# A one-layer hybrid encoder step on eight cores: the division of each attention head in three spread steps, and another plan for the bf16 weight copies

## The chip, the cores and the metric

The kernel runs on all 8 NeuronCores of one Trainium2 chip. Cores 0 to 3 form one die, cores 4 to 7 the other. Each core has a matrix engine (TensorE, PE in the rows), a vector engine (VectorE, DVE), an activation engine (ScalarE, ACT), GpSimd (POOL) and a sync engine (SyncE, SP), and 16 DMA engines that all of its DMA queues share. The metric is the device time in microseconds of the slowest core for one launch. Every core does the same amount of work on its own data; there is no traffic between cores.

## The reference, cut to what matters

One layer is computed for 4 prompts of 8192 frames and 32 running streams of 16 new frames:

```
xn = rms_norm(x);  q,k,v,u,vb,gA,gB = split(xn @ w_in)            # 2048 -> 9216
A  = softmax(q.k/sqrt(128) + bias, own 64-chunk + 8 before) @ v   # 8 heads of 128
S  = gelu(u) * (causal(w_s) @ rms_norm(gelu(vb)) + b_s)           # 128-frame chunks
x  = x + (sigmoid(gA)*(A @ w_branch_a) + sigmoid(gB)*(S @ w_branch_b)) @ w_out
h  = conv3(rms_norm(x) @ w_up);  x = x + (gelu(h_gate)*h_val) @ w_down  # 2 x 5632 wide
y  = rms_norm(x)
```

K and V rows, the normalised rows of the spatial gate and the last rows ahead of the convolution are returned too. All weights arrive as f32.

## The kernel before, in words

**Tiles.** A core takes 4096 prompt frames (half of a prompt, with 576 frames of halo) and 4 of the 32 running streams. It works through its frames in 8 tiles of 512 frames. Tile 0 also carries 66 extra columns (64 frames of the running streams, 2 halo columns), so that most of its matmuls come in two sets of 289 columns where later tiles have one of 512. All activations are feature-major: features on partitions, frames along the free axis. In each tile the stages follow one another: `vb` and `u` with the spatial gate; attention, with q, k, v projections as filler; the merge of both branches (`merge`); the output projection (`out_proj`); the FFN (`ffn`), which does `w_up` in two parts (24 and 20 blocks), each followed by its half of `w_down` (16 blocks each). Tile 0 has the halo and the running streams besides.

**Order of the work.** The class `Sched` records operations in program order, one in-order list for each engine, and derives the semaphore waits from the keys that they read and write. Nothing is reordered: what an engine meets in its list is what it waits for. `mm` (line 394) issues every matmul, `Sched.dma` (line 93) every DMA.

**Weights.** `wload` brings one weight block (up to 128 partitions x 4096 bf16, 1 MiB) into the next slot of a ring `wbuf` of 5 slots; in the FFN of tile 0 the ring has 7 (two in `wx_sb`). There are 136 blocks, numbered `bi` in the order of first use: 0 to 19 are q, k, v, u and vb; 20 to 51 the merge, in fours (gate A, gate B, `w_a`, `w_b`; the last two are 512 KiB); 52 to 59 `w_out`; 60 to 83 and 100 to 119 `w_up` (1 MiB each); 84 to 99 (768 KiB) and 120 to 135 (640 KiB) `w_down`. A block is used once per tile. Until a bf16 copy of it lies in the DRAM scratch `wscr`, it is loaded from the f32 original `wblk` with a casting DMA on GpSimd's queue. Once the copy is there, it is loaded from `wscr` on SP's queue. `keeps(rk, bi, uses)` (line 417) decides at each casting load whether the block is also stored to `wscr` after it has landed: `uses` is 0 in tile 0, 1 in tile 1, and in tile 2 whatever is left is stored. The store is queued on SP two `wload`s later (`flush_stores`), and the next load into the same slot waits for it. The merge asks for blocks in the order gate A, gate B, `w_a`, `w_b`, and uses them in the order gate A, `w_a`, gate B, `w_b`, for each of the two feature chunks of a step; 8 steps make a merge.

**Attention.** `attention_run` walks over 64 items, 8 key blocks for each of 8 heads. An item's front (`attn_front`) is the score matmul, a bias add on VectorE (line 851) and an exponential on ScalarE (line 854) into `pbf`; its back (`attn_back`), two items later, is the product with V into the bank `ob` and the row sum (product with ones) into the bank `db`. Items are 128, 256, 384, 512, 512, 384, 256 and 128 columns wide. Behind the items the generator `fillers` gives out portions of 4 matmuls of the q, k, v and first gate projections, paced by `total`; `ready(h)` pulls q and k of a head ahead of its first item. After a head's last item `finish_head` divides: ScalarE takes Ln of `db` (line 826), copies `ob` (line 827), takes Exp(-Ln) (line 828), and GpSimd multiplies (line 833; VectorE in tile 0). The banks alternate, (6, 7) for even heads and (2, 3) for odd ones. `next_norm` loads the next tile's x in pieces (`xst`, on ScalarE's DMA queue) during the second part of the FFN; its squares (line 490) and their matmuls (`Stats`) stand between the FFN's. `xst` has 2 slots in tile 0 and 4 later.

Of the kernel before, what the change touches and what calls it, by code (L numbers as in the profile page):

```python
# [207 lines left out]
def build(n_main=8, do_ext=True):  # L208
    nc = bass.Bass("TRN2", target_bir_lowering=False)
    S = Sched(nc)  # L210
# [42 lines left out]
    sb = nc.alloc_sbuf_tensor  # L253
# [42 lines left out]
    act = RA.tensor("act_sb", [128, 32, WIDE], BF16, 0)  # L296
# [49 lines left out]
    honesb = sb("honesb_sb", [128, 128], BF16)  # L346
    onesD = sb("onesD_sb", [128, 128], BF16)
    hist = sb("hist_sb", [128, 88, 2], F32)
    cols = sb("cols_sb", [128, 64], F32)
    print("[build] sbuf bytes remaining", nc.sbuf_bytes_remaining, flush=True)  # L350

    ps = [nc.alloc_psum_tensor(f"ps{i}", [128, 512], F32) for i in range(8)]
# [25 lines left out]
    def X(k):  # L378
        return RX.keys(("x", k))

    def XE(k):
        return RT.keys(("xe", k))

    def A(s):
        return RA.keys(("act", s))

    def pk(b):
        return [("ps", b)]
# [4 lines left out]
    def mm(b, out, lhsT, rhs, start, stop, reads, skip=False):  # L393
        S.op("pe", lambda e: e.matmul(out, lhsT, rhs, start=start, stop=stop, skip_group_check=skip),  # L394
             reads=reads, writes=pk(b))
# [21 lines left out]
    def keeps(rk, bi, uses):  # L417

        if uses == 0:
            return (rk[0] == "w_in" and rk[3] < 5120) or bi % 4 == 0  # L420
        if uses == 1:
            return bi % 4 == 1 or bi % 8 == 3
        return True

    def wload(tag, k0, k1, c0, c1, after=()):
        ap, wkeys, sid = wring["slots"][st["wb"] % len(wring["slots"])]
        st["wb"] += 1
        nk = k1 - k0
        ncol = c1 - c0
        assert nk * ncol <= 4096  # L430
        n = nk * ncol
        flat = ap[:, 0:n]
        view = flat.rearrange("p (k c) -> p k c", c=ncol)
        rk = (tag, k0, k1, c0, c1)
        if rk not in scr_idx:
            scr_idx[rk] = len(scr_idx)
            assert scr_idx[rk] < NBLK
            BLOCKS.append(rk)
        bi = scr_idx[rk]
        uses = scr_state.get(rk, 0)  # L440
        wring["n"] += 1
        flush_stores(2)
        if uses == "kept":
            S.dma("sp", flat, wscr[bi, :, 0:n], reads=[("scr",) + rk], writes=wkeys, sem=("wb", sid))
        else:
            S.dma("pool", flat, wblk_d[bi, :, 0:n], reads=after, writes=wkeys, sem=("wbc", sid))
            if keeps(rk, bi, uses):
                pend_store.append((wring["n"], bi, flat, wkeys, sid, rk, n))
                scr_state[rk] = "kept"
            else:  # L450
                scr_state[rk] = uses + 1
        return view, wkeys
# [369 lines left out]
    def finish_head(T, ob, db, dst, dkeys, view=None, eng="pool"):  # L822
        t = next_tmp()
        t2 = next_tmp()
        n = T
        S.op("act", lambda e: e.activation(tmpf[:, t, 0:n], ps[db][:, 0:n], AF.Ln), reads=pk(db), writes=[("tmpf", t)])  # L826
        S.op("act", lambda e: e.copy(tmpf[:, t2, 0:n], ps[ob][:, 0:n]), reads=pk(ob), writes=[("tmpf", t2)])
        S.op("act", lambda e: e.activation(tmpf[:, t, 0:n], tmpf[:, t, 0:n], AF.Exp, scale=-1.0),  # L828
             reads=[("tmpf", t)], writes=[("tmpf", t)])
        a0, a1 = tmpf[:, t2, 0:n], tmpf[:, t, 0:n]  # L830
        if view is not None:
            a0, a1 = view(a0), view(a1)
        S.op(eng, lambda e: e.tensor_tensor(dst, a0, a1, ALU.mult), reads=[("tmpf", t2), ("tmpf", t)], writes=dkeys)

    def attention_items(h, b0, masked_halo):
        items = []
        for kb in range(b0 - 4, b0 + 4):
            c0 = max(2 * kb, 2 * b0)
            c1 = min(2 * kb + 9, 2 * (b0 + 4) - 1)
            items.append(dict(h=h, kb=kb, q0=64 * (c0 - 2 * b0), nq=64 * (c1 - c0 + 1), m0=64 * c0 - 128 * kb, sl=ring_slot(kb),  # L840
                              first=kb == b0 - 4, last=kb == b0 + 3, ones=honesb if masked_halo and kb < 0 else onesb,
                              okey="honesb" if masked_halo and kb < 0 else "onesb", eng="dve" if masked_halo else "pool",
                              banks=(6, 7) if masked_halo or h % 2 == 0 else (2, 3)))
        return items

    def attn_front(n, it):
        h, sl, q0, nq, m0 = it["h"], it["sl"], it["q0"], it["nq"], it["m0"]
        sbk = AT_S[n % 2]
        mm(sbk, ps[sbk][:, 0:nq], KT[:, h, sl * 128:(sl + 1) * 128], act[:, h, q0:q0 + nq], True, True, [("KT", h, sl)] + A(h))
        t = next_tmp()  # L850
        S.op("dve", lambda e: e.scalar_tensor_tensor(tmpf[:, t, 0:nq], ps[sbk][:, 0:nq], 60.0, TB[:, h, m0:m0 + nq],  # L851
                                                     ALU.min, ALU.add), reads=pk(sbk) + TBK[h], writes=[("tmpf", t)])
        p = next_pb()
        S.op("act", lambda e: e.activation(pbf[:, p, 0:nq], tmpf[:, t, 0:nq], AF.Exp), reads=[("tmpf", t)], writes=[("pb", p)])  # L854
        it["p"] = p

    def attn_back(it):
        h, sl, q0, nq, p = it["h"], it["sl"], it["q0"], it["nq"], it["p"]
        ob, db = it["banks"]
        mm(ob, ps[ob][:, q0:q0 + nq], VR[:, sl, h * 128:(h + 1) * 128], pbf[:, p, 0:nq], it["first"], False,  # L860
           [("VR", sl, h // 4), ("pb", p)], skip=True)
        mm(db, ps[db][:, q0:q0 + nq], it["ones"][:], pbf[:, p, 0:nq], it["first"], False, [it["okey"], ("pb", p)], skip=True)
        if it["last"]:
            finish_head(512, ob, db, act[:, 24 + h, 0:512], A(24 + h), eng=it["eng"])

    def attention_run(b0, first, gen, total, state, v1_late):

        cnt = {"pulled": 0, "items": 0, "end": False}

        def pull():  # L870
            if next(gen, "end") == "end":
                cnt["end"] = True
            cnt["pulled"] += 1

        def after_item():
            cnt["items"] += 1
            want = total(cnt["items"])
            while cnt["pulled"] < want and not cnt["end"]:
                pull()

        def ready(h):
            while not (("q", h) in state["have"] and ("k", h) in state["have"]):
                pull()
            while h >= 4 and v1_late and not state["v1"]:
                pull()

        items = sum([attention_items(h, b0, first) for h in range(NH)], [])
        LA = 2
        for n in range(len(items) + LA):
            if n >= LA:  # L890
                attn_back(items[n - LA])
            if n < len(items):
                ready(items[n]["h"])
                attn_front(n, items[n])
            if n >= LA:
                after_item()
            else:
                pull()
        while not cnt["end"]:
            pull()  # L900

# [601 lines left out]
```

How the kernel before makes its waits and increments, by code:

```python
        def run(e, eng):  # L160
            es = eng_sem[e]
            for op in self.ops[e]:
                for sem, val in op.waits:
                    eng.wait_ge(sem, val)
                ins = op.fn(eng)
                if op.signal:
                    ins.then_inc(es, 1)
                if op.dma_key is not None:
                    ins.then_inc(dma_sem[op.dma_key], 16)
            if e == "sp":
                for sem, val in final_waits:
                    eng.wait_ge(sem, val)
```

## Time and profile before

| | |
|---|---|
| median of 3 runs | 7616.94 us (7616.44 to 7643.23) |
| the profiled execution, its own time | 7632.61 us |
| its span, slowest core (core 6) | 7631.1 us |
| spans of the 8 cores | 7589.3 to 7631.1 us |
| mean granted TensorE clock | 0.973 to 0.975 of full |
| TensorE / VectorE / ScalarE / GpSimd busy | 95% / 42% / 27% / 3% |
| chain that ended last | PE 85%, DMA 7%, DVE 3%, issue 2%, ACT 2% |
| HBM read, written | 1351.36 MB, 165.86 MB |
| casting loads of weights / stores to `wscr` | 267 / 136 |

All rows are of core 6, the slowest. A row of `--windows` form gives for each stretch each engine's busy time, the granted TensorE clock (1.00 is 2.4 GHz), the share of the time that the 16 DMA engines were busy, and GB/s. Matmuls are pipelined, so that a busy PE says that no gap was seen, not that it ran at its peak. Sizes in the DMA rows are those at the bf16 end.

### The profile page before, as it was taken

How to read it: one execution, taken by the hardware profiler on the slowest of the kernel's cores; microseconds unless marked ns; L12 is line 12 of the kernel's file. 1: busy time of each engine (PE TensorE's matmuls, PEld its weight loads, DVE VectorE, ACT ScalarE, POOL GpSimd, SP SyncE). 2: the span in 40 equal slices, each digit the busy share in tenths (PEclk: the TensorE clock that was granted, in tenths of full speed). 3: DMA queues.
4: the chain of work that ended last, by engine and by line, in shares of the span. 5: the costliest groups of instructions: out<-in, count | busy, mean ns of one | idle time of the engine just before them, and what ended most of it. 6: DMA issues, size and time to landing. Idle time of an engine off the chain costs nothing.

```text
span 7631.1 us, 105163 instructions; the slowest of 8 cores (7589.3 to 7631.1 us)
## 1 busy us (share of the span) xinstructions
PE 7246.9 (95%) x36913; PEld 3544.6 (46%) x36913; DVE 3172.7 (42%) x5494; ACT 2067.2 (27%) x4598; POOL 225.7 (3%) x368
## 2 busy tenths in 40 slices
PE   8889999889988999989999999999999999999998
PEld 4567775334433444434444444444444444444443
DVE  3314764226342264423553244522644235532544
ACT  1412332213223132231332232331322222322322
POOL 0000000000000000000000000000000000000000
PEclk9989999999998999999999999999999999999999
DMA  8879897389983779824455344534456344563443
GB/s 204 156 162 174 163 183 211 105 179 210 208 217 112 176 203 232 242 93 157 147 180 198 116 153 160 192 136 158 141 180 211 100 155 150 182 206 120 156 150 137
DMA packets 268578, 1281.08 MB, mean 168 GB/s; under 512 B 32672, under 2 KB 38304, under 8 KB 166560
## 3 DMA queue, kind: packets, MB, share of 16 engines
q1 hardware_dynamic: 186160, 964.99, 37.9%
q0 software_dynamic: 44720, 243.03, 20.1%
q10 hardware_dynamic: 37184, 66.34, 2.8%
q8 instruction: 307, 5.03, 0.3%
q14 instruction: 207, 1.70, 0.1%
HBM read 1351.36 MB, written 165.86 MB: 199 GB/s over the span
## 4 chain that ended last, share of the span: by engine, by line
PE 85%; DMA 7%; DVE 3%; issue 2%; ACT 2%; SPq 0%; DVEq 0%; ACTq 0%; POOLq 0%; POOL 0%
PE ps L394 85%; DMA wbuf_sb<-wblk 3%; DMA wbuf_sb<-wscr 2%; DMA xst_sb<-xT 1%; DVE tmpf_sb L1173 1%; ACT pbf_sb L854 1%; DVE tmpf_sb L851 1%; DMA VC_sb<-cv 1%; SPq L93 0%; DVE tmpf_sb L1259 0%; ACT tmpf_sb L828 0%; ACT tmpf_sb L826 0%; DVE act_sb L1228 0%; DVE tas_sb L1200 0%; DVE xn_sb L531 0%
## 5 line engine op out<-in xcount | busy, mean ns | idle before, releaser
L394 PE MATMUL ps<-xn_sb,wbuf_sb 128*128 128x512 bf16 (+1 forms) x19968 | 4095.9, 363 | 17.4 <-DMA wbuf_sb<-wblk 10.3
L394 PEld LDWEIGHTS ps<-xn_sb,wbuf_sb 128*128 128x128 bf16 x19968 | 1941.5, 98 | 2038.0 <-issue 53.6
L394 PE MATMUL ps<-act_sb,wbuf_sb 128*128 128x512 bf16 (+2 forms) x10552 | 2186.3, 363 | 96.8 <-DMA wbuf_sb<-wblk 78.5
L394 PEld LDWEIGHTS ps<-act_sb,wbuf_sb 128*128 128x128 bf16 x10552 | 1024.6, 97 | 1193.5 <-issue 140.8
L1173 DVE SCALAR_TENSOR_TENSOR tmpf_sb<-tmpf_sb,convp_sb 128x512 f32<-128x512 f32 x1408 | 1052.1, 748 | 112.5 <-ACT tmpf_sb L1165 29.0
L1259 DVE TENSOR_TENSOR tmpf_sb<-ps,rinv_sb 128x512 f32<-128x512 f32 (+2 forms) x792 | 500.5, 632 | 606.9 <-PE ps L394 595.4
L1133 DVE TENSOR_TENSOR tmpf_sb<-ps,tmpf_sb 128x512 f32<-128x512 f32 (+1 forms) x288 | 181.6, 639 | 1185.0 <-PE ps L394 1184.8
L1165 ACT COPY tmpf_sb<-hist_sb 128x2 f32<-128x2 f32 x704 | 134.9, 192 | 1625.7 <-DVE tmpf_sb L1259 1606.8
L1167 ACT ACTIVATE tmpf_sb<-tmpf_sb,convp_sb 128x512 f32<-128x512 f32 x704 | 571.4, 812 | 0.7
L1292 DVE TENSOR_TENSOR xT_sb<-ps,xT_sb 128x512 f32<-128x512 f32 (+2 forms) x288 | 181.8, 632 | 900.7 <-PE ps L394 897.5
L1128 ACT ACTIVATE tmpf_sb<-ps 128x512 f32<-128x512 f32 (+1 forms) x288 | 156.6, 556 | 1250.4 <-PE ps L394 1250.4
L394 PE MATMUL ps<-wbuf_sb,xn_sb 128*128 128x512 bf16 (+1 forms) x2112 | 478.0, 383 | 12.6 <-DMA wbuf_sb<-wscr 8.8
L851 DVE SCALAR_TENSOR_TENSOR tmpf_sb<-ps,TB_sb 128x128 f32<-128x128 f32 (+3 forms) x512 | 247.0, 491 | 535.7 <-PE ps L394 504.5
L854 ACT ACTIVATE pbf_sb<-tmpf_sb 128x128 bf16<-128x128 f32 (+3 forms) x512 | 234.2, 469 | 390.2 <-DVE tmpf_sb L851 302.0
L394 PEld LDWEIGHTS ps<-wbuf_sb,xn_sb 128*128 128x128 bf16 (+1 forms) x2112 | 207.0, 99 | 253.2 <-issue 23.7
L394 PE MATMUL ps<-pbf_sb,VR_sb 128*128 128x128 bf16 (+3 forms) x512 | 177.3, 346 | 143.9 <-ACT pbf_sb L854 138.1
L1228 DVE TENSOR_TENSOR act_sb<-tmpf_sb 128x512 bf16<-128x512 f32 x352 | 243.5, 692 | 32.8 <-DVE tmpf_sb L1173 0.9
L1177 ACT ACTIVATE tmpf_sb<-tmpf_sb 128x512 f32<-128x512 f32 x352 | 222.1, 631 | 102.2 <-DVE tmpf_sb L1173 101.6
L490 ACT ACTIVATE pbf_sb<-xT_sb 128x512 bf16<-128x512 f32 x136 | 85.5, 630 | 507.3 <-DVE xT_sb L1292 317.4
L1154 DVE TENSOR_TENSOR xT_sb<-ps,xT_sb 128x512 f32<-128x512 f32 (+2 forms) x144 | 91.1, 633 | 280.9 <-PE ps L394 279.3
L394 PE MATMUL ps<-pbf_sb,onesD_sb 128*128 128x512 bf16 (+2 forms) x464 | 141.7, 364 | 69.4 <-ACT pbf_sb L490 41.3
L1158 ACT ACTIVATE xn_sb<-xT_sb,gcols_sb 128x512 bf16<-128x512 f32 x128 | 92.4, 722 | 399.5 <-DVE xT_sb L1154 393.1
(130 smaller groups left out, 2720.6 us busy)
## 6 DMA issues: line engine op xcount, KB each, us to landing
wbuf_sb<-wscr SPq DMA_DIRECT2D x549, 1024.0 KB, 5.9
wbuf_sb<-wblk POOLq DMA_DIRECT2D x143, 1024.0 KB, 15.3
wscr<-wbuf_sb SPq DMA_DIRECT2D x84, 1024.0 KB, 12.4
wbuf_sb<-wscr SPq DMA_DIRECT2D x94, 768.0 KB, 4.4
wbuf_sb<-wscr SPq DMA_DIRECT2D x94, 640.0 KB, 4.8
xst_sb<-xT ACTq DMA_DIRECT2D x224, 256.0 KB, 4.9
wbuf_sb<-wscr SPq DMA_DIRECT2D x84, 512.0 KB, 5.3
xT_sb<-xT SPq DMA_DIRECT2D x144, 256.0 KB, 10.4
```

Source lines behind the costliest of these rows:

```text
L394: S.op("pe", lambda e: e.matmul(out, lhsT, rhs, start=start, stop=stop, skip_group_check=skip), reads=reads, writes=pk(b))
L851: S.op("dve", lambda e: e.scalar_tensor_tensor(tmpf[:, t, 0:nq], ps[sbk][:, 0:nq], 60.0, TB[:, h, m0:m0 + nq], ALU.min, ALU.add), reads=pk ...
L854: S.op("act", lambda e: e.activation(pbf[:, p, 0:nq], tmpf[:, t, 0:nq], AF.Exp), reads=[("tmpf", t)], writes=[("pb", p)])
L1128: S.op("act", lambda e, b=b, t=t, n=n: e.activation(tmpf[:, t, 0:n], ps[b][:, 0:n], AF.Sigmoid), reads=pk(b), writes=[("tmpf", t)])
L1133: S.op("dve", lambda e, b=b, t=t, n=n: e.tensor_tensor(tmpf[:, t, 0:n], ps[b][:, 0:n], tmpf[:, t, 0:n], ALU.mult), reads=pk(b) + [("tmpf", ...
L1165: S.op("act", lambda e: e.copy(tmpf[:, th, 0:2], hist[:, c, :]), reads=[("hist", c)], writes=[("tmpf", th)])
L1167: S.op("act", lambda e: e.activation(tmpf[:, ta, 0:512], tmpf[:, th, 2:514], AF.Identity, bias=convp[:, c, 3:4], scale=convp[:, c, 2:3]), ...
L1173: S.op("dve", lambda e, tap=tap: e.scalar_tensor_tensor(tmpf[:, ta, 0:512], tmpf[:, th, tap:tap + 512], convp[:, c, tap:tap + 1], tmpf[:, ...
L1177: S.op("act", lambda e: e.activation(tmpf[:, ta, 0:512], tmpf[:, ta, 0:512], AF.Gelu), reads=[("tmpf", ta)], writes=[("tmpf", ta)])
L1228: S.op("dve", lambda e: e.tensor_tensor(act[:, slot, 0:512], tmpf[:, t0, 0:512], tmpf[:, ta, 0:512], ALU.mult), reads=[("tmpf", t0), ("tmp ...
L1259: S.op("dve", lambda e, th=th, b=b, a=a, m=m, off=off: e.tensor_tensor(tmpf[:, th, 2 + a:2 + a + m], ps[b][:, off:off + m], rinv[:, a:a + ...
L1292: S.op("dve", lambda e, ap=ap, b=b, off=off, m=m: e.tensor_tensor(ap, ps[b][:, off:off + m], ap, ALU.add), reads=pk(b) + ky, writes=ky)
```

## The change

Two edits. In the first, the division of a head in tiles 1 to 7 (`it["eng"]` is not `"dve"`) isn't done at once any more. `close_steps` puts three operations on a list: Ln of `db` into a new tile `dinv` (2 KiB of each partition), Exp(-x) on `dinv`, and on VectorE the product of the bank `ob` with `dinv` into `act`. `attention_run` takes one from the list after each following `attn_front`, and what is left after the last item. The copy of `ob` on ScalarE and the product on GpSimd are gone, and so are two slots of `tmpf` for each head. Tile 0 keeps `finish_head`. In the second, `keeps` decides otherwise.

```
-            return (rk[0] == "w_in" and rk[3] < 5120) or bi % 4 == 0
+            if rk[0] in ("w_up", "w_down"):
+                return bi % 9 in (0, 2, 4, 6)
+            return rk[3] < 5120 and rk[0] == "w_in" or bi % 4 == 0
         if uses == 1:
-            return bi % 4 == 1 or bi % 8 == 3
+            return bi % 9 in (1, 5) if rk[0] in ("w_up", "w_down") else bi % 4 == 2
```
```
         if it["last"]:
-            finish_head(512, ob, db, act[:, 24 + h, 0:512], A(24 + h), eng=it["eng"])
+            if it["eng"] == "dve":
+                finish_head(512, ob, db, act[:, 24 + h, 0:512], A(24 + h), eng="dve")
+            else:
+                close_steps(h, ob, db)
+    def close_steps(h, ob, db):
+        closing.append(lambda: S.op("act", lambda e: e.activation(dinv[:], ps[db][:, 0:512], AF.Ln), reads=pk(db), writes=["dinv"]))
+        closing.append(lambda: S.op("act", lambda e: e.activation(dinv[:], dinv[:], AF.Exp, scale=-1.0), reads=["dinv"],
+                                    writes=["dinv"]))
+        closing.append(lambda: S.op("dve", lambda e: e.tensor_tensor(act[:, 24 + h, 0:512], ps[ob][:, 0:512], dinv[:], ALU.mult),
+                                    reads=pk(ob) + ["dinv"], writes=A(24 + h)))
```
```
                 attn_front(n, items[n])
+            if closing and n < len(items):
+                closing.pop(0)()
...
+        while closing:
+            closing.pop(0)()
```

Counted out from the code, block by block (MiB at the bf16 end; casting loads / stores):

| | before | after |
|---|---|---|
| tile 0, FFN | 76 casts 66 MiB / 19 stores 16.5 MiB | 76 casts 66 MiB / 34 stores 29.6 MiB |
| tile 1, merge | 23 casts 15 MiB / 11 stores 9 MiB | 23 casts 15 MiB / 8 stores 4 MiB |
| tile 1, `w_out` | 6 casts / 3 stores | 6 casts / 2 stores |
| tile 1, FFN | 57 casts 49.5 MiB / 28 stores 24.3 MiB | 42 casts 36.4 MiB / 16 stores 14.1 MiB |
| tile 2, merge | 12 casts 6 MiB / 12 stores 6 MiB | 15 casts 11 MiB / 15 stores 11 MiB |
| tile 2, `w_out` | 3 casts / 3 stores | 4 casts / 4 stores |
| tile 2, FFN | 29 casts 25.3 MiB / 29 stores | 26 casts 22.3 MiB / 26 stores |

The rest of tile 0 is as before. In the merge of tile 1 gate B, `w_a` and `w_b` come by casting loads before and after; gate B and every other `w_b` were stored there before, and `w_a` is now. In the merge of tile 2 the casting loads were `w_a` and every other `w_b`, and are gate B and `w_b` now. Over the whole run there are 267 casting loads before and 254 after, and 136 stores in both.

## Rows read from the trace of the kernel before

**Rows 1.** The page, its part 1: busy us, share of the span, instructions of each engine.
```profile
PE 7246.9 (95%) x36913; PEld 3544.6 (46%) x36913; DVE 3172.7 (42%) x5494; ACT 2067.2 (27%) x4598; POOL 225.7 (3%) x368
```

**Rows 2.** Windows: the FFN of tiles 0, 1, 2, 3, a stretch a row.
```profile
706.00:1255.00 549.00, 540.04 (x4272) 417.64 (x4272) 358.21 (x994) 188.88 (x586) 37.53 (x71) 1.00 0.90 174
1730.00:2238.00 508.00, 473.56 (x2141) 208.79 (x2142) 247.58 (x357) 149.79 (x347) 28.54 (x54) 0.97 0.98 207
2694.00:3161.00 467.00, 462.90 (x2145) 206.97 (x2144) 249.64 (x358) 149.70 (x347) 14.27 (x27) 1.00 0.87 220
3594.00:4058.00 464.00, 462.73 (x2144) 207.03 (x2144) 248.99 (x358) 149.93 (x347) 0.00 (x0) 1.00 0.51 168
```

**Rows 3.** Windows: the merge of tiles 1, 2 and 4.
```profile
1462.00:1672.00 210.00, 175.43 (x771) 75.87 (x770) 32.40 (x47) 22.31 (x37) 14.89 (x27) 0.95 0.72 160
2437.00:2634.00 197.00, 176.23 (x772) 76.33 (x771) 32.37 (x48) 22.31 (x37) 8.52 (x15) 0.95 0.64 161
4256.00:4423.00 167.00, 166.97 (x774) 74.44 (x773) 32.80 (x49) 22.31 (x37) 1.09 (x1) 1.00 0.46 142
```

**Rows 4.** Windows: attention items of tile 5, first to last bias add.
```profile
5024.00:5143.00 119.00, 101.13 (x481) 45.72 (x479) 34.61 (x69) 47.05 (x98) 7.63 (x7) 0.89 0.23 80
```

**Rows 5.** Waits of PE over the span: us in total, times, longest us.
```profile
PE ps L394 <- ACT pbf_sb L854: 138.1, 150, 1.7
PE ps L394 <- DMA wbuf_sb<-wblk: 92.6, 27, 6.4
PE ps L394 <- ACT pbf_sb L490: 41.3, 30, 8.5
```

**Rows 6.** DMA queues, 706 to 1255 us (FFN of tile 0): packets, MB, share; then issues, KB, us to landing.
```profile
q0 software_dynamic: 10486, 65.84, 74.0%
...
wbuf_sb<-wblk POOLq DMA_DIRECT2D x27, 1024.0 KB, 16.6
...
xst_sb<-xT ACTq DMA_DIRECT2D x32, 256.0 KB, 7.2
```

**Rows 7.** The same, 1730 to 2238 us (FFN of tile 1).
```profile
wscr<-wbuf_sb SPq DMA_DIRECT2D x15, 1024.0 KB, 14.2
...
xst_sb<-xT ACTq DMA_DIRECT2D x32, 256.0 KB, 20.6
```

**Rows 8.** The same, 3594 to 4058 us (FFN of tile 3).
```profile
q1 hardware_dynamic: 10944, 69.21, 44.8%
```

**Rows 9.** Timeline of ACT, 5082 to 5085 us of tile 5, where head 4 begins.
```profile
5082.62 0.58 ACT L826 ACTIVATE tmpf_sb<-ps 128x512 f32<-128x512 f32 x1
5083.09 0.58 ACT L827 COPY tmpf_sb<-ps 128x512 f32<-128x512 f32 x1
5083.56 0.64 ACT L828 ACTIVATE tmpf_sb<-tmpf_sb 128x512 f32<-128x512 f32 x1
5084.09 0.83 ACT L854 ACTIVATE pbf_sb<-tmpf_sb 128x256 bf16<-128x256 f32 x2
```

**Rows 10.** Timeline of PE, the same head: the products with V that had to wait.
```profile
5084.65 0.27 PE L394 MATMUL ps<-pbf_sb,VR_sb 128*128 128x256 bf16 x1 [1.35 <-ACT pbf_sb L854]
5087.03 0.58 PE L394 MATMUL ps<-pbf_sb,VR_sb 128*128 128x512 bf16 x1 [1.25 <-ACT pbf_sb L854]
```

**Rows 11.** Timeline of PE, the first of these places where head 3 begins.
```profile
5062.51 0.27 PE L394 MATMUL ps<-pbf_sb,VR_sb 128*128 128x256 bf16 x1 [0.41 <-ACT pbf_sb L854]
```

**Rows 12.** Windows of 3.4 us behind the place of rows 9.
```profile
5084.20:5087.60 3.40, 1.70 (x8) 0.76 (x9) 1.30 (x2) 1.98 (x4) 1.09 (x1) 0.83 0.00 0
5087.60:5091.00 3.40, 2.79 (x11) 0.96 (x9) 0.98 (x2) 0.94 (x2) 0.00 (x0) 0.50 0.02 5
5091.00:5094.40 3.40, 3.40 (x13) 1.37 (x12) 0.29 (x1) 0.31 (x1) 0.00 (x0) 0.67 0.00 0
```

**Rows 13.** Groups by line: the product on VectorE with the bank as input, and the GpSimd product.
```profile
L1133 DVE TENSOR_TENSOR tmpf_sb<-ps,tmpf_sb 128x512 f32<-128x512 f32 (+1 forms) x288 | 181.6, 639 | 1185.0 <-PE ps L394 1184.8
...
L833 POOL TENSOR_TENSOR act_sb<-tmpf_sb 128x512 bf16<-128x512 f32 x56 | 61.0, 1090 | 1155.2 <-ACT tmpf_sb L828 1155.2
```

More of the change, by code:

```diff
@@ L348, in build @@
     hist = sb("hist_sb", [128, 88, 2], F32)
+    dinv = sb("dinv_sb", [128, 512], F32)
     cols = sb("cols_sb", [128, 64], F32)
@@ L863, in attn_back @@
         if it["last"]:
-            finish_head(512, ob, db, act[:, 24 + h, 0:512], A(24 + h), eng=it["eng"])
+            if it["eng"] == "dve":
+                finish_head(512, ob, db, act[:, 24 + h, 0:512], A(24 + h), eng="dve")
+            else:
+                close_steps(h, ob, db)
+    closing = []
+    def close_steps(h, ob, db):
[4 more added lines that the diff above has]
+                                    reads=pk(ob) + ["dinv"], writes=A(24 + h)))
     def attention_run(b0, first, gen, total, state, v1_late):
```

## The prediction

> **What bounds the kernel now.** I read four views, in this order. The page's busy line says that TensorE is busy for 95% of the span [rows 1]; the stages are the same in every tile, so a tile without trouble is the yardstick for the others. The windows give it: the FFN takes 464 us in tile 3, 467 in tile 2 and 508 in tile 1 [rows 2]; the merge takes 167 us in tile 4, 197 in tile 2 and 210 in tile 1 [rows 3]. So tile 1 loses 44 us in its FFN and 43 in its merge, tile 2 3 us and 30. The reader is to see the last but one column beside it: the DMA engines are busy for 0.98 of tile 1's FFN, 0.87 of tile 2's, 0.51 of tile 3's, but only for 0.72 and 0.64 of the two merges. The FFN of tile 1 is short of DMA time, the merges are short of slots: each of their 8 steps waits for one late block, and TensorE is idle for 35 and 21 us in them. The waits of PE name the third loss [rows 5]: 138 us for the exponentials of attention, the largest entry. It is the same in every tile: in tile 5 TensorE is idle for 18 of 119 us, and the granted clock is 0.89 [rows 4]. Tile 0's FFN already has its DMA engines at 0.90 [rows 2].
>
> **DMA prices.** In tile 0's FFN the casting queue moved 65.84 MB in 74.0% of 549 us [rows 6]: 406 us, or 6.17 us/MB, 6.5 us of all 16 engines for 1 MiB. Plain transfers took 44.8% of 464 us for 69.21 MB in tile 3 [rows 8]: 208 us, 3.0 us/MB, 3.15 us for 1 MiB. I price a store like a load, since that row holds only loads.
>
> **FFN of tile 1: 40 us won.** 13.1 MiB of casting loads become plain loads: 13.1 x (6.5 - 3.15) = 44 us of DMA time less. 10.2 MiB of stores go: 32 us. The demand falls from 0.98 x 508 = 498 us to 422 us, against 464 us of matmuls: share 0.91. Tile 0 shows 549 us at 0.90 with 9 us of PE idle, tile 2 467 us at 0.87 with 4 [rows 2]. So of the 44 us lost some 4 stay. Bounds: 35 and 44.
>
> **FFN of tile 0: 10 us lost.** 13.1 MiB of stores come on top: 41 us. The demand goes from 0.90 x 549 = 494 us to 535 us, share 0.975, and the stage is 549 us long because of its matmuls. In the sum it still fits. It fits badly: the stores fall evenly, but the second part has the `xst` loads too, and `w_down` uses a MiB in less matmul time than `w_up`. The ring of 7 slots takes up some of it. Bounds: 0, if the ring hides all, and 44, what tile 1 loses at 0.98 with 5 slots. I take 10, nearer to the first, since the demand in sum stays under the matmul time while tile 1's was 34 us over it. What would be late first is `xst`: 7.2 us from issue to landing here [rows 6], 20.6 where the engines are full [rows 7].
>
> The Trainium skill ("DMA: Bandwidth & Descriptors", SWDGE vs HWDGE vs iDMA) says that each DMA engine takes turns between the queues that feed it; this speaks against the change, for a store would slow the casts beside it before the engines are full. By that rule a cast in tile 0 would land later than the 16.6 us of rows 6 towards the 14 to 21 us transfers of rows 7; no row before shows tile 0 with the added stores. It raises the chance of the second rival below, not its price.
>
> **Merges.** In tile 1 the casting loads are the same; the 8 stores of gate B (1 MiB) and 4 of `w_b` are replaced by 8 of `w_a` (0.5 MiB): 5 MiB less. Gate B's slot takes the next `w_a`, the block that each step waits for, and its store competes with that load. The wait per step is 35/8 = 4.3 us; a store less of 1 MiB is 3.15 us of DMA time, of which I let a third show: 8 us won; bounds 0 and 8 x 2.5 = 20, more than half of the wait. In tile 2, `w_a`, now the late block of every step, comes as a plain load, but gate B and all `w_b` are casts, 5 MiB more, and are stored. Gate B's load starts when the slot of gate A is free, two thirds through a step of 167/8 = 20.9 us [rows 3], and is wanted 5 us into the next: 12 us, where a 1 MiB cast took 16.6 from issue to landing [rows 6]. One late block takes the place of the other: 3 us a step now, 3 us after. I take 0; bounds are -32 (5 MiB x 6.5, all shown) and +30 (all of 197 - 167). `w_out` of tile 2 has one cast more: -1. The FFN of tile 2 has 3 MiB fewer casts and stores (19 us of DMA time); it lost 3 us and wins them: 3.
>
> **Division: 28 us won.** Before, the order on ScalarE is Exp of the next head's first item, then Ln, copy and Exp(-Ln) of the head that ends, 0.58 + 0.58 + 0.64 = 1.8 us, then Exp of the second item [rows 9], for which TensorE has waited 1.35 us [rows 10]. After, Ln stands behind the second item's Exp, Exp(-x) behind the third's, the product on VectorE behind the fourth's bias add; the copy and GpSimd's 1.09 us [rows 13] are gone. Where q, k, v fillers stand between the items (heads 1 to 3), the wait was 0.41 us [rows 11], and it goes: 3 x 0.41 a tile. In heads 4 to 7 the items run without filler, since `ready` pulled q and k ahead in one piece, and each item hangs on score, bias add and Exp in turn. Followed through from rows 9 and 10: the second product with V comes at 83.3 instead of 84.65, the third is then held by its own chain, and the fourth has 0.4 us of Exp(-x) ahead of it: 86.1 instead of 87.0. The product, 0.64 us by a like row on VectorE with a bank as input [rows 13], holds the fifth's bias add for 0.35 us. So 1.35 us are won and about half is given back: 0.7 us a head, 4 heads a tile. Per tile 2.8 + 1.2 = 4.0, over 7 tiles 28 us. Bounds: 28 x 1.35 + 21 x 0.41 = 46, and -2, if the 0.58 + 0.64 + 0.64 = 1.86 us of the moved operations all stand on the chain in 28 heads where 1.8 stood. After the last head the closing comes at once, 0.4 us shorter than GpSimd's; fillers cover it. A bank is held two items longer; its next head comes after 8 more items. `dinv` is read out well before its next use. Ln and Exp alternate as in rows 9, which show no table load between them.
>
> **The clock.** Behind the place of rows 9 the granted clock is 0.83, 0.50, 0.67 in three windows of 3.4 us [rows 12]: 6.8 us at 1.2 GHz after a stretch in which TensorE was busy for 1.70 of 3.4 us. That is once per head in heads 4 to 7, 28 times in tiles 1 to 7. The stretch ahead hardly gets denser: about 2800 instead of 2700 columns in the 3.4 us before the fall, counted from the replay. So I leave the clock as it is.
>
> The Trainium skill ("TensorE: Matmul & The Clock Gate", HAM oscillation) prices throttled time at half of it, 3.4 us for each of these stretches; rows 12 would give less, since part of the 6.8 us is idle anyway. The page's figure makes the whole worth 28 x 3.4 us, the first rival's upper end.
>
> **Sum.** 40 - 10 + 8 + 0 - 1 + 3 + 28 = 68 us. The profiled execution took 7632.6 us, its span 7631.1; it becomes 7565. It is 15.7 us above the median of the runs, 7616.9; I take the 68 us from the median: **7549 us**, 0.9% faster. The likeliest case's own range is 7510 to 7580.
>
> **Rivals.**
> 1. *The clock stays up in attention.* If the earlier second product suffices, 6.8 us at half clock go in up to 28 places. At most 28 x 3.4 = 95 us, half of it if half of the places go: 7549 - 47 = 7502 to 7454. For it: TensorE's load ahead of the fall does rise. Against: the items remain without fillers, and that is what thins it.
> 2. *Tile 0's DMA engines fill up* and its FFN loses what tile 1's lost, 44 instead of 10: 7583. For it: 0.90 and 41 us more. Against: the slots are 7, and the matmul time is longer by 85 us than in tile 1.
> 3. *The division was hidden or is merely moved*: its 28 us become 0 (the lower bound, -2): 7577.
> 4. *Slower: the filler-less items turn out to be bound by ScalarE and VectorE.* Then the spread operations hold up three items instead of one, 28 x 1.86 us, with 38 us of burst gone; and the thinner matmuls double the stretch at half clock from 6.8 to 13.6 us, 28 x 3.4 = 95 us. Attention then costs 52 - 38 + 95 = 109 us, the weight plan gives 40: 7617 + 69 = 7686. It decides from 40 us lost in attention, 1.4 us a head, on. Against: ScalarE is busy for 1.98 and 0.94 of 3.4 us there, VectorE for 1.30 and 0.98 [rows 12].
>
> **How the numbers follow.** Forecast 0.60; rival 1 0.12; rival 2 0.16; rival 3 0.06; rival 4 0.06. What a measurement can tell here is about 0.5%, 38 us: faster means below 7579. The forecast is there but for 0.03, rival 1 is, rival 3 half, rival 2 for a third (0.05): 0.57 + 0.12 + 0.03 + 0.05 = 0.77. Slower 0.06, the rest, 0.17, the same. The range for 8 in 10 takes in rival 2 and the nearer half of rival 1, and leaves out the far half of it and rival 4: 7490 to 7598.
>
> **What would show it.** FFN of tile 1 at 466 to 470 us with a DMA share near 0.91; FFN of tile 0 at 550 to 570 us with a share near 0.97, and `xst` landing later there; merge of tile 1 near 202 us, of tile 2 near 197, with gate B the block waited for; the wait for line 854 down from 138 us to some 100; GpSimd without its product; four stretches of 6.8 us at half clock in each tile still there. The prediction is wrong if tile 0's FFN goes over 580 us, if tile 2's merge goes over 210, or if the windows of attention keep 119 us.

## The result, and the profile after

The kernel after took 7550.27 us (median of 5 runs) against 7616.94 before; the ratio of the runs that can be compared is 0.9897, 95% interval 0.9879 to 0.9914. A second measurement (`e11_after_again`, below) gave 0.9918 (0.9887 to 0.9948). The quotient of the two medians is 0.9912, and the forecast, 7549 us, is 0.9911 of 7617. The total was met; most of its terms were not, and their errors offset each other (see the table further below).

Windows of the kernel after, core 6 (busy us and count of PE, PEld, DVE, ACT, POOL, then granted clock, DMA share, GB/s): the FFN of tiles 0, 1 and 2, the merge of tile 1, `w_out` of tile 1, the merges of tiles 2 and 4, and the attention items of tile 5. They answer to [rows 2], [rows 3] and [rows 4].

```profile
688.00:1254.00 566.00, 542.28 (x4255) 417.94 (x4271) 358.41 (x992) 189.30 (x585) 38.12 (x72) 0.99 0.95 193
1707.00:2171.00 464.00, 460.29 (x2100) 206.84 (x2142) 249.07 (x357) 150.34 (x347) 21.24 (x40) 1.00 0.87 199
2630.00:3094.00 464.00, 460.30 (x2102) 206.93 (x2144) 249.59 (x357) 150.35 (x347) 12.74 (x24) 1.00 0.83 218
1450.00:1645.00 195.00, 174.47 (x757) 75.87 (x771) 33.42 (x49) 22.33 (x37) 12.74 (x24) 0.95 0.67 137
1645.00:1707.00 62.00, 58.81 (x261) 25.98 (x265) 21.46 (x31) 10.86 (x15) 2.65 (x5) 0.97 0.93 206
2363.00:2573.00 210.00, 181.20 (x759) 77.92 (x774) 33.80 (x50) 22.19 (x37) 8.50 (x16) 0.90 0.61 163
4165.00:4333.00 168.00, 167.20 (x761) 75.07 (x775) 33.56 (x50) 22.41 (x37) 0.00 (x0) 0.99 0.43 141
4934.00:5045.00 111.00, 98.02 (x471) 44.07 (x479) 39.18 (x76) 44.40 (x90) 0.00 (x0) 0.94 0.24 86
```

The reader is to see four changes: the FFN of tile 1 has its yardstick length of 464 us, tile 0's has grown from 549 to 566, the merge of tile 2 has grown from 197 to 210 although tile 1's fell from 210 to 195, and attention takes 111 us at a granted clock of 0.94, where it took 119 at 0.89.

The waits of PE, core 6 (us in total, times, longest): the one for exponentials is 113 us, 138 before [rows 5], the one for casting loads is 45 us, 93 before, and the one for plain loads has grown to 38 us. The last line is that of the kernel before.

```profile
PE ps L395 <- ACT pbf_sb L857: 113.4, 161, 1.7
PE ps L395 <- DMA wbuf_sb<-wblk: 44.8, 18, 5.9
PE ps L395 <- DMA wbuf_sb<-wscr: 37.6, 14, 5.6
PE ps L394 <- DMA wbuf_sb<-wscr: 26.3, 15, 6.1
```

Since the stages are the same in every kernel, all runs can be set side by side. The table has the mean length in us over cores 4 to 7, cut at the first and last instruction of each stage's own line (attention: mean of tiles 1 to 6, first to last bias add; half clock: time at 1.2 GHz in attention, tiles 1 to 7, summed). The ratio is that of a kernel's time to the time of the kernel before, measured beside it. Each row's stages come from one profiled execution. The rows `after` and `e11` are the same kernel and differ by up to 5.3 us in a stage, so a difference of that size in one cell says nothing by itself.

| kernel | ratio (95%) | attention | half clock | FFN 0 | merge 1 | `w_out` 1 | FFN 1 | merge 2 | FFN 2 |
|---|---|---|---|---|---|---|---|---|---|
| before | 1 | 118.5 | 189 | 551.3 | 214.5 | 57.3 | 509.6 | 196.3 | 465.4 |
| after | 0.9897 (0.9879-0.9914) | 111.7 | 91 | 567.6 | 192.8 | 63.9 | 464.1 | 205.0 | 465.0 |
| e1 division alone | 0.9914 (0.9899-0.9929) | 111.6 | 88 | 546.8 | 202.5 | 57.7 | 509.8 | 185.7 | 466.2 |
| e2 plan alone | 0.9970 (0.9942-0.9998) | 118.2 | 180 | 571.2 | 205.2 | 64.0 | 464.1 | 217.5 | 464.0 |
| e3 FFN plan only | 0.9901 (0.9876-0.9926) | 111.7 | 82 | 572.1 | 202.3 | 57.7 | 464.5 | 183.0 | 464.3 |
| e4 burst | 1.0011 (1.0000-1.0023) | 123.8 | 172 | 574.4 | 197.2 | 64.0 | 464.6 | 211.1 | 464.0 |
| e5 pace | 0.9796 (0.9764-0.9828) | 102.0 | 16 | 566.6 | 194.4 | 64.3 | 464.0 | 208.4 | 464.5 |
| e6 merge kept | 0.9867 (0.9828-0.9906) | 112.0 | 103 | 567.2 | 209.1 | 68.8 | 464.1 | 172.2 | 464.0 |
| e7 tile 0, part 2 | 0.9947 (0.9914-0.9981) | 111.8 | 96 | 558.2 | 193.2 | 64.1 | 470.0 | 210.4 | 494.2 |
| e8 spread, GpSimd | 0.9919 (0.9894-0.9943) | 110.6 | 71 | 567.8 | 205.7 | 65.3 | 464.2 | 215.9 | 464.1 |
| e9 both | 0.9764 (0.9740-0.9789) | 102.1 | 17 | 570.7 | 211.6 | 69.6 | 464.1 | 168.6 | 464.0 |
| e10 thirds | none | 102.0 | 19 | 564.3 | 212.6 | 68.7 | 480.9 | 165.8 | 464.0 |
| e11 after again | 0.9918 (0.9887-0.9948) | 111.6 | 84 | 572.9 | 192.2 | 64.2 | 464.2 | 210.3 | 464.0 |

Some executions of every kernel ran much slower, with one die or both at a lower clock; ratios leave them out, and for e10 there is none.

### The profile page after: what moved, and what is told of

It reads as the page before. It is cut to its first block, busy times and chain, and to the rows that moved or that the text cites. A ratio compares the mean times of both kernels' runs of the same rounds, so it can differ in the third digit from the quotient of the medians.

```text
span 7548.4 us, 104076 instructions; the slowest of 8 cores (7519.0 to 7548.4 us)
## 1 busy us (share of the span) xinstructions
PE 7191.6 (95%) x36305; PEld 3537.4 (47%) x36913; DVE 3209.2 (43%) x5550; ACT 2048.7 (27%) x4542; POOL 158.3 (2%) x299
## 4 chain that ended last, share of the span: by engine, by line
PE 86%; DMA 5%; DVE 4%; issue 2%; ACT 2%; SPq 0%; DVEq 0%; ACTq 0%; POOLq 0%
PE ps L395 86%; DMA wbuf_sb<-wscr 2%; DMA wbuf_sb<-wblk 2%; DVE tmpf_sb L1193 1%; DVE tmpf_sb L854 1%; ACT pbf_sb L857 1%; DMA xst_sb<-xT 1%; DMA VC_sb<-cv 0%; DVE tmpf_sb L1279 0%; SPq L93 0%; DVE act_sb L1248 0%; DVE tas_sb L1220 0%; ACT dinv_sb L877 0%; ACT pbf_sb L493 0%; DVE xn_sb L534 0%
## 5 line engine op out<-in xcount | busy, mean ns | idle before, releaser
L395 PE MATMUL ps<-pbf_sb,onesD_sb 128*128 128x512 bf16 (+3 forms) x433 | 133.3, 361 | 58.4 <-ACT pbf_sb L493 31.8
## 6 DMA issues: line engine op xcount, KB each, us to landing
wbuf_sb<-wblk POOLq DMA_DIRECT2D x140, 1024.0 KB, 14.1
```

## The experiments

### e1 and e2: one edit at a time

e1 is the kernel after with the old rule of `keeps`; e2 the kernel before with the new one.

> The spread division with the weight plan of before. Theory: the two edits add up, and the division is worth more than was forecast, because it lifts the granted clock too: the attention items take 112 us a tile instead of 118.7, 6.5 us over 7 tiles, so 7617 - 45 = 7572 us (7562 to 7582), with 260 to 300 us at half clock on a core instead of 386. Rival: the division is only moved and the whole gain is the weight plan's: 7610 to 7617, attention at 118 us.

> The weight plan with the division of before. Theory: FFN of tile 1 at 464 to 467 us (44 won), FFN of tile 0 17 us longer, merge of tile 1 near 195, merge of tile 2 near 210 (12 lost), w_out of tile 1 some 5 us longer: about 67 - 45 = 22 us won in all, 7595 us (7583 to 7603). Rival (the forecast's sizes): 40 us won, 7577. Rival that the division carries everything: 7617.

Division alone 0.9914, plan alone 0.9970; the sum of both gains, 1.16%, is within the intervals of the 1.03% of both together. So most of the gain is the division's: 0.0086 of 7617 us are 66 us, and the plan's 0.0030 are 23 us, where the forecast had 28 and 40. e1's time at half clock over the whole span, 276 us on the mean of cores 4 to 7, is within the expected 260 to 300. With the division attention takes 111.6 us, with or without the plan. The merges show why it is worth more than attention's 6.9 us a tile: with the division alone tile 1's falls by 12 us and tile 2's by 11. The same windows as in [rows 3], in e1 (tile 1, tile 2):

```profile
1452.00:1654.00 202.00, 177.65 (x761) 77.00 (x776) 34.04 (x51) 22.27 (x37) 12.67 (x24) 0.94 0.71 161
2416.00:2600.00 184.00, 169.05 (x754) 74.46 (x769) 33.02 (x48) 22.08 (x37) 6.34 (x12) 0.98 0.58 155
```

and the merge of tile 2 in e2:

```profile
2411.00:2629.00 218.00, 189.06 (x781) 80.78 (x795) 37.04 (x54) 20.83 (x34) 8.98 (x17) 0.90 0.67 176
```

The plan alone costs 21 us there. The 8.7 us more of the kernel after are the sum of +21 and -11, which nobody sees in the total.

### e3: gate B and `w_b` not left for tile 2

```
-            return bi % 9 in (1, 5) if rk[0] in ("w_up", "w_down") else bi % 4 == 2
+            return bi % 9 in (1, 5) if rk[0] in ("w_up", "w_down") else bi % 4 == 1 or bi % 8 == 3
```

> The kernel after, but blocks outside w_up and w_down are stored in tile 1 by the rule of before (gate B and every other w_b instead of w_a). Theory: in tile 2 the casts of gate B and w_b slow the plain load of w_a beside them; with them gone the merge of tile 2 falls from 209 to about 197 us, the merge of tile 1 rises from 195 to about 210, w_out of tile 1 falls by 5: in sum 7548 us (7540 to 7556). Rival: the merge of tile 2 stays at 209, since its loss comes from the FFN plan: 7565.

The merge of tile 2 falls to 183.0 us, further than expected, and `w_out` of tile 1 to 57.7; the merge of tile 1 rises to 202.3. By these three stages that is 22 + 6 - 10 = 18 us for e3; its FFN 0 is 4.5 us longer in this execution, as it is in e11, with the same plan there. The ratios, 0.9901 and 0.9897, don't tell the two kernels apart, so that a gain of e3 in the total is not shown. The loss in tile 2 is the rule for the merge blocks, not the FFN's.

### e4: the three operations at once

```
                 close_steps(h, ob, db)
+                while closing:
+                    closing.pop(0)()
```

> The kernel after, but the three closing operations are issued at once behind the last item, as before, so that only the copy and the GpSimd product are gone. Theory: what counts is where they stand. The burst ahead of the second item's Exp is 1.2 us instead of 1.8, so a third of the attention's gain stays: 7550 + 30 = 7580 us (7570 to 7590), half-clock time near 350 us. Rival: the missing copy and the bank's earlier release are what counts: 7550.

Both theories were too kind: attention takes 123.8 us, 5 more than before the change, and the ratio is 1.0011. The copy and the GpSimd product are gone here as well, so that it is the spreading that wins, and it has to win back what the move to VectorE costs in a burst. (The time at half clock over the whole span is 363 us, near the 350 expected.) The timeline of e4 where head 4 of tile 5 begins, DVE:

```profile
5074.88 0.29 DVE L854 SCALAR_TENSOR_TENSOR tmpf_sb<-ps,TB_sb 128x128 f32<-128x128 f32 x1 [7.21 <-PE ps L395]
5076.88 0.69 DVE L881 TENSOR_TENSOR act_sb<-ps,dinv_sb 128x512 bf16<-128x512 f32 x1 [1.71 <-ACT dinv_sb L879]
5077.49 0.88 DVE L854 SCALAR_TENSOR_TENSOR tmpf_sb<-ps,TB_sb 128x256 f32<-128x256 f32 x2
```

and PE:

```profile
5078.56 0.37 PE L395 MATMUL ps<-pbf_sb,VR_sb 128*128 128x256 bf16 x1 [2.39 <-ACT pbf_sb L857]
```

VectorE waits 1.71 us for the Exp in front of its product, and the bias add of the second item, which needs nothing of it, is queued behind. TensorE waits 2.39 us, where it waited 1.35 with GpSimd taking that wait [rows 10].

### e5: fillers between the items of heads 4 to 7

```
-        attention_run(b0, False, fillers(), lambda n: (7 * 8 + 16 + 8 - 4) * n / 64, state, True)
+        attention_run(b0, False, fillers(), lambda n: 1.5 * n if n < 32 else 48 + 0.9 * (n - 32), state, True)
```

> The kernel after, with another pace of the fillers in tiles 1 to 7: 1.5 portions for an item up to item 32 and 0.9 from there, so that heads 4 to 7 keep fillers between their items. Theory: the idle time and the half clock of attention come from items without fillers. Then the half-clock time of attention in tiles 1 to 7 falls from 75 us to under 20 and its idle time from 14 us a tile to under 7, and 8 to 12 us a tile go, 7550 - 70 = 7480 us (7465 to 7495). Rival: each item hangs on score, bias add and Exp in any case, and fillers only move the wait: 7550.

The theory holds in its main numbers: the ratio is 0.9796, where 7480 of 7617 is 0.982; the fast executions took 7453 to 7492 us; half clock is 16 us in place of 91, and attention 102.0 us, 9.7 less. One number was missed: TensorE is still idle for about 8 us a tile in attention (8.3 on the mean of cores 4 to 7, 101.0 - 93.5 in the window below), where under 7 was expected. The window and the wait of tile 5 in e5 (the columns of [rows 4] and [rows 5]):

```profile
4894.00:4995.00 101.00, 93.50 (x489) 44.86 (x487) 39.11 (x76) 44.22 (x91) 0.00 (x0) 1.00 0.27 94
```
```profile
PE ps L395 <- ACT pbf_sb L857: 6.9, 10, 0.9
```

### e6: all merge blocks stored in tile 1

```
-            return bi % 9 in (1, 5) if rk[0] in ("w_up", "w_down") else bi % 4 == 2
+            return bi % 9 in (1, 5) if rk[0] in ("w_up", "w_down") else True
```

> The kernel after, but every block outside w_up and w_down that is cast in tile 1 is also stored there, so that tile 2 casts none of them. Theory: the merge of tile 2 falls from 209 to under 172 us and its w_out to 57; the merge of tile 1, with 11 MiB of stores more at a DMA share of some 0.65, rises from 195 to about 207, w_out and FFN of tile 1 by up to 10: 7550 - 15 = 7535 us (7522 to 7548). Rival: the stores hold the slots, each step of tile 1 waits for them, its merge goes to 230, and nothing is won.

Its merges (tile 1, then tile 2, core 6):

```profile
1448.00:1660.00 212.00, 180.78 (x776) 77.21 (x773) 33.60 (x50) 22.30 (x37) 12.74 (x24) 0.92 0.76 178
2380.00:2549.00 169.00, 167.19 (x775) 74.10 (x774) 33.55 (x50) 22.30 (x37) 0.00 (x0) 1.00 0.44 139
```

Tile 2 wins 33 us (mean of the four cores), tile 1 loses 16 in the merge and 5 in `w_out`: 12 us for e6. The ratio 0.9867 is lower than 0.9897, but the intervals overlap: the total leaves open whether e6 is faster than the kernel after. The 33 us in tile 2 are far beyond what repeats differ by.

### e7: fewer stores in the second part of tile 0's FFN

```
-                return bi % 9 in (0, 2, 4, 6)
+                return bi % 9 in (0, 2, 4, 6) if bi < 100 else bi % 4 == 0
```

> The kernel after, but blocks 100 and up (second part of the FFN) are stored in tile 0 by the rule of before, every fourth. Theory: the 17 to 20 us that this part of tile 0 lost come from the added stores beside the xst loads; w_up part 2 of tile 0 falls from 192 to 171 to 176 us, while tile 1's second part has 6 MiB more to cast and loses up to 12 us: 7550 - 8 = 7542 us (7532 to 7552). Rival: the loss comes from the stores of the first part, whose backlog arrives there: no change in the 192 us.

The second `w_up` part of tile 0 takes 177.8 us before, 192.9 after, 184.9 in e7: roughly half of its loss goes with its own stores, and the rest stays. That the rest comes from the stores of the first part, as the rival said, is not shown; no run leaves out those alone. I had missed the price: the blocks not stored in tiles 0 and 1 are cast and stored in tile 2, 17.6 MiB in the second part of its FFN instead of 9.8, and that FFN goes from 465 to 494 us. By stages e7 is some 25 us slower than the kernel after; its ratio, 0.9947, lies above both measurements of that kernel, but its interval overlaps that of the second one.

### e8: spread, but with copy and GpSimd

```
-        closing.append(lambda: S.op("dve", lambda e: e.tensor_tensor(act[:, 24 + h, 0:512], ps[ob][:, 0:512], dinv[:], ALU.mult),
-                                    reads=pk(ob) + ["dinv"], writes=A(24 + h)))
+        def product():
+            t = next_tmp()
+            S.op("act", lambda e: e.copy(tmpf[:, t, 0:512], ps[ob][:, 0:512]), reads=pk(ob), writes=[("tmpf", t)])
+            S.op("pool", lambda e: e.tensor_tensor(act[:, 24 + h, 0:512], tmpf[:, t, 0:512], dinv[:], ALU.mult),
+                 reads=[("tmpf", t), "dinv"], writes=A(24 + h))
+        closing.append(product)
```

> The kernel after, but the third step is the copy on ScalarE and the product on GpSimd, as before the change, only spread. Theory: GpSimd's product of the last head stands in its in-order list ahead of the casting loads of the merge, and holds them until attention ends. Then the first merge step of tiles 1 and 2 goes back from 21 to 30 us, and attention stays near 113: 7550 + 20 = 7570 us (7562 to 7580). Rival: the order in time of the product has no part in the merges, and the first step stays at 21 to 23 us: 7552.

Attention is 110.6 us, so GpSimd does no harm there. With before and e4 this makes four cases: at once with GpSimd 118.5 us, at once with VectorE 123.8, spread with GpSimd 110.6, spread with VectorE 111.7. Spreading wins in both pairs; the move to VectorE costs a little in attention. The merges go back up, to 205.7 and 215.9 us. POOL at the start of tile 1's merge in e8:

```profile
1472.36 1.09 POOL L882 TENSOR_TENSOR act_sb<-tmpf_sb,dinv_sb 128x512 bf16<-128x512 f32 x1 [5.25 <-ACT tmpf_sb L881]
1475.50 1.13 POOL L93 DMA_DIRECT2D wbuf_sb<-wblk  x2 [2.05 <-PE ps L395]
```

and PE:

```profile
1483.49 4.91 PE L395 MATMUL ps<-act_sb,wbuf_sb 128*128 128x512 bf16 x16 [8.90 <-DMA wbuf_sb<-wblk]
```

The casting loads of the first `w_a` and `w_b` are issued 2 us behind the product of the last head, which ends attention, and TensorE waits 8.9 us for them. In the kernel after, POOL has no product; the same two loads are issued as soon as their slots are free, 36 and 12 us ahead of the end of attention (at 1450.7 there), and TensorE's first wait for a cast in that merge is 1.85 us, one step later:

```profile
1414.24 0.53 POOL L93 DMA_DIRECT2D wbuf_sb<-wblk  x1 [5.46 <-PE ps L395]
1439.09 0.53 POOL L93 DMA_DIRECT2D wbuf_sb<-wblk  x1 [24.32 <-PE ps L395]
```
```profile
1475.41 1.89 PE L395 MATMUL ps<-act_sb,wbuf_sb 128*128 128x512 bf16 x8 [1.85 <-DMA wbuf_sb<-wblk]
```

The first of the 8 steps, counted from the last bias add of attention, takes on the mean of cores 4 to 7 30.6 us (tile 1) and 30.5 (tile 2) before, 21.6 and 22.5 after, and 31.7 and 26.7 in e8. The theory holds in tile 1 in full, in tile 2 for part; what else raises e8's merge of tile 2 to 216 us was not followed up.

### e9 to e11: the best version, and a control

e9 joins the edits of e5 and e6. e10 adds `((0, 2, 4, 6) if bi < 100 else (0, 2, 4))` and `((1, 5) if bi < 100 else (1, 5, 6))`.

> The pace of e5_pace and the stores of e6_merge_kept together. Theory: they work at different places and add up: attention at 101 to 104 us a tile, merge of tile 2 at 169, merge of tile 1 near 210; 7481 - 20 = 7461 us (7448 to 7475), ratio 0.977. Rival: with attention shorter, the DMA engines of tiles 1 and 2 have less time and take the gain of the merge back: 7481.

> e9_both, but of the FFN's second part a third of the blocks is stored in each of tiles 0, 1 and 2. Theory: w_up part 2 of tile 0 falls from 193 to about 186 us, since its loss goes with its own stores, and tiles 1 and 2 stay without a loss of more than 4 us: 5 us faster than e9_both. Rival: tile 2, with 12 blocks more or less, loses as it did when only a quarter was stored in tile 0: slower than e9_both by 5 us or more.

> The kernel after once more, beside the two above on the same chip. Both theories: the same ratio as first measured, 0.990, with attention at 112 us a tile, w_up part 2 of tile 0 at 192, merge of tile 2 at 208.

e9 beats both kernels: its ratio to before is 0.9764 (0.9740 to 0.9789), from two executions, where 0.977 was expected. By stages the gains add up: attention takes 102.1 us as in e5, the merge of tile 2 168.6 as in e6. In the total e9 and e5 (0.9796) are not told apart. e10 shows no gain: tile 0's FFN is 6 us shorter, tile 1's 17 longer (I had allowed 4), tile 2's the same, and its profiled execution took 7466.1 us, that of e9 7465.7. The control repeats the stages of the kernel after within 6 us.

## Why the prediction was right, term by term

In us won, by cores 4 to 7 of the table: forecast, measured.

| term | forecast | measured |
|---|---|---|
| FFN of tile 1 | 40 | 45.5 |
| FFN of tile 0 | -10 | -16 |
| merge of tile 1 | 8 | 22 (plan 9, division 12) |
| `w_out` of tile 1 | 0 | -7 |
| merge of tile 2 | 0 | -9 (plan -21, division +11) |
| `w_out` and FFN of tile 2 | 2 | about 0 |
| attention, 7 tiles | 28 | 7 x 6.8 = 48 |
| sum | 68 | 84 |

**The total, right, and its closeness luck.** The forecast was 7549 us and 7550.3 came, and two lucky circumstances made it that close. First, the errors of the terms cancel between the edits: the plan was forecast at 40 us and is worth 23 (e2), the division at 28 and is worth 66 (e1). Second, the forecast took its 68 us, read from a profiled execution of 7632.6 us, off a median that is 15.7 us lower. The two profiled executions differ by 82 us (7632.6 and 7550.3), which the stages' 84 account for; the medians differ by 67.

**FFN of tile 1, right.** The demand was to fall to a share of 0.91; the window has 0.87. The two queues' rows of the kernel after in that window (packets, MB, share):

```profile
q0 software_dynamic: 5760, 36.05, 49.3%
q1 hardware_dynamic: 7415, 47.51, 30.6%
```

49.3% of 464 us for 36.05 MB are 6.3 us/MB, 30.6% for 47.51 MB 3.0: the prices of the forecast, stores included, hold. The forecast didn't say what TensorE waited for in this stage before. For the most part it was no weight: of 34 us idle (core 6, 1730:2238) 23.5 were for ScalarE's squares of the next tile's x, whose pieces took 20.6 us to land [rows 7] and take 8.1 after. In the kernel after that wait is gone.

```profile
PE ps L394 <- ACT pbf_sb L490: 23.5, 3, 8.5
```

On the mean of cores 4 to 7, 29 us of this stage were at half clock before and none after.

**FFN of tile 0, right in kind, off in size.** 0.95 x 566 = 538 us of DMA time; 535 were forecast. PE idle went from 9 to 24 us. The demand fits, yet the transfers land later: a 1 MiB cast took 16.6 us before [rows 6] and takes 23.1 with the added stores (DMA issues of that window, core 6):

```profile
wbuf_sb<-wblk POOLq DMA_DIRECT2D x28, 1024.0 KB, 23.1
wscr<-wbuf_sb SPq DMA_DIRECT2D x14, 1024.0 KB, 14.4
```

The Trainium skill ("DMA: Bandwidth & Descriptors", SWDGE vs HWDGE vs iDMA) says that a DMA engine takes turns between the queues that feed it. The later landings fit that, but the trace doesn't separate it from engines that are simply full for a time: their share is 90% or more in 33 of 40 slices of this stage.

The whole loss is in the second `w_up` part, and there TensorE waits for no weight block. It waits for the squares of x, as in tile 1 before. The forecast's sign, that `xst` would be late first, came true: a piece takes 13.3 us to land there, 7.2 before. Waits in that part, core 6, after (981:1174) and, last line, before (999:1174):

```profile
PE ps L395 <- ACT pbf_sb L493: 9.2, 3, 5.3
ACT pbf_sb L493 <- DMA xst_sb<-xT: 31.5, 6, 8.7
ACT pbf_sb L490 <- DMA xst_sb<-xT: 7.3, 2, 4.2
```

On the mean of cores 4 to 7 the waits for squares in this FFN went from 2.4 to 11.8 us and the time at half clock from 0 to 12. The forecast had no term for the clock here.

**Merge of tile 2, wrong.** The step that failed is "One late block takes the place of the other: 3 us a step now, 3 us after." I had set the plain load of `w_a` as no longer late and gate B's cast as late. The wait of PE is for `w_a`, now a plain load: it waits 27.3 us in 7 steps for `wbuf_sb<-wscr`, 3.9 a step. Issues in the merge of tile 2 after, and in the second block those of e6, where no cast is left in this merge:

```profile
wbuf_sb<-wblk POOLq DMA_DIRECT2D x9, 1024.0 KB, 9.8
...
wbuf_sb<-wscr SPq DMA_DIRECT2D x7, 512.0 KB, 8.6
```
```profile
wbuf_sb<-wscr SPq DMA_DIRECT2D x14, 512.0 KB, 5.6
```

The load of `w_a` is issued when the casts of gate B and `w_b` are in flight, and takes 8.6 us instead of the 5 its place allows; without casts beside it it takes 5.6. Most steps then take 27 us instead of 24. (The forecast had set over 210 us for this merge as a sign of being wrong: core 6 stands at 210, the mean of four cores at 205, e11 at 210.3.) The clock adds to it: on core 6 the granted clock of the merge is 0.90, 0.95 before [rows 3], and of its 13 us more 8 are idle time and 5 busy time of TensorE. e6 takes the casts away, and 172 us remain; e3 turns them round (`w_a` and half of `w_b` are cast, gate B is plain), and 183 remain.

**`w_out` of tile 1, missed.** It is 7 us longer with the new rule for the blocks outside the FFN (e1 and e3 57.7, e2 64.0). I had looked at its store saved, not at where the stores stand in SyncE's list. SyncE, before (the merge ends at 1672.5), then after (it ends at 1645.8):

```profile
1674.91 0.32 SPq L93 DMA_DIRECT2D wscr<-wbuf_sb  x1
1675.39 0.40 SPq L93 DMA_DIRECT2D wbuf_sb<-wscr  x1
```
```profile
1653.58 0.32 SPq L93 DMA_DIRECT2D wscr<-wbuf_sb  x1
1654.10 0.32 SPq L93 DMA_DIRECT2D wbuf_sb<-wscr  x1
```

and PE after:

```profile
1675.96 5.30 PE L395 MATMUL ps<-act_sb,wbuf_sb 128*128 128x512 bf16 x16 [2.92 <-DMA wbuf_sb<-wscr]
```

The plain load of block 56 stands behind a store in both. The store waits until its block has landed. Before it is block 53's, by the new rule block 54's, whose cast lands later, so that the load is issued 8.3 us into the stage instead of 2.9. It takes 22 us to land (the DMA share of the stage is 0.93), and TensorE waits 2.9 us for it on this core. Over cores 4 to 7 the wait is 4.6 us and 5 us are at half clock; before there was neither. No run moves this store alone.

**Division: the mechanism right, two steps wrong.** The replay (the forecast's item by item count for one head) was close. Head 4 of tile 5 after, ACT:

```profile
5021.62 0.84 ACT L857 ACTIVATE pbf_sb<-tmpf_sb 128x128 bf16<-128x128 f32 x2 [0.73 <-DVE tmpf_sb L854]
5022.37 0.58 ACT L876 ACTIVATE dinv_sb<-ps 128x512 f32<-128x512 f32 x1
5023.35 0.53 ACT L857 ACTIVATE pbf_sb<-tmpf_sb 128x384 bf16<-128x384 f32 x1 [0.40 <-DVE tmpf_sb L854]
5023.78 0.61 ACT L877 ACTIVATE dinv_sb<-dinv_sb 128x512 f32<-128x512 f32 x1
```

PE:

```profile
5022.61 0.27 PE L395 MATMUL ps<-pbf_sb,VR_sb 128*128 128x256 bf16 x1
5024.02 0.32 PE L395 MATMUL ps<-pbf_sb,VR_sb 128*128 128x384 bf16 x1 [0.82 <-ACT pbf_sb L857]
5025.06 0.58 PE L395 MATMUL ps<-pbf_sb,VR_sb 128*128 128x512 bf16 x1 [0.34 <-ACT pbf_sb L857]
```

The second product with V has no wait (1.35 us before), the third waits on its own chain, the fourth comes 4.2 us after the head's first score matmul (at 5020.9), where it took 5.4 [rows 10] against a forecast of 4.5. The step that failed is "So I leave the clock as it is." The time at half clock in attention fell from 189 to 91 us. Behind this head it is still there (windows as in [rows 12]):

```profile
5024.40:5027.80 3.40, 2.74 (x8) 0.57 (x6) 1.84 (x3) 1.41 (x3) 0.00 (x0) 0.54 0.00 0
5027.80:5031.20 3.40, 2.79 (x9) 1.16 (x10) 0.72 (x2) 1.00 (x3) 0.00 (x0) 0.50 0.02 7
5031.20:5034.60 3.40, 3.40 (x16) 1.50 (x15) 0.00 (x0) 0.60 (x1) 0.00 (x0) 0.96 0.06 10
```

but not behind every head: 13 us a tile are at half clock, where four stretches of 6.8 were to remain. So the first rival was in part the truth: 14 us a tile less at half clock. What that is worth is told by cores 5 and 7, whose profiles have every matmul in both kernels: over tiles 1 to 7 their attention fell by 47 us, TensorE's idle time by 30, its busy time by 17 (which is the clock). The 30 are the forecast's 28; the 17 were forecast as nothing. The rival had priced half of the places at 47 us, which was too much: 85 us less at half clock gave 17.

The other failed step cost GpSimd's product at nothing. Its busy time is nothing, but with its wait it stood ahead of the casting loads in GpSimd's list. The division's edit took 11 to 12 us out of each of two merges, 8 to 9 of them in the first step. e8, which puts the product back, returns 13 us in tile 1; in tile 2 it returns 11 against the kernel after, but 6 against its repetition e11, so that there the cause is shown only in part.

## What to carry to other kernels

An operation that waits costs its place in an in-order list, not its duration: the same three instructions are worth -5 us a tile in a burst and +7 spread behind items that don't need them, and a 1.1 us product that waits on GpSimd can hold a DMA issue for as long as it waits. The same holds for a store on SyncE that waits for its block: the load behind it is late (`w_out`). A plain load beside two casts was a late load (8.6 us against 5.6). Where a stage runs short of DMA time, look at what TensorE waits for: here it was the next tile's x, not the weights. And idle time was paid twice here: in attention, in the merge of tile 2, in `w_out` and in the FFN of tile 0 time at half clock came with it, and went with it. Before moving what stands between items, look at whether the items have fillers at all: changing one line of pace (e5, 0.9897 to 0.9796) won as much again as the whole change.

## What the hardware showed that I had not expected

A casting load takes the 16 engines about twice as long per byte at the bf16 end as a plain one (6.3 against 3.0 us/MB). Its landing time can grow while the engines' mean share does not: in the second `w_up` part of tile 0 the share is 0.91 before and after, and a 1 MiB cast lands after 14.4 us and after 23.1.

How the granted clock answers was not found. The windows of 3.4 us that end where it falls behind head 4 of tile 5, before and after:

```profile
5083.01:5086.41 3.40, 1.43 (x9) 0.50 (x7) 1.55 (x3) 2.06 (x6) 1.09 (x1) 1.00 0.00 0
5021.25:5024.65 3.40, 1.77 (x10) 0.67 (x9) 2.10 (x5) 2.51 (x6) 0.00 (x0) 1.00 0.00 0
```

TensorE was busy for 1.43 us of the one and 1.77 of the other, and the clock fell behind both. (The forecast's 1.70 is of a window that already holds 1.2 us at half clock.) Over all heads, about half of the time at 1.2 GHz went.
